# K with Q and V with U in one transformer block: four projections by seven block products each instead of eight

## The chip, the cores and the metric

The kernel runs on one core of a Trainium2 chip. The metric is the device time of one execution in microseconds (us), the median of several runs. Times in the trace are counted from the first instruction of one profiled execution. TensorE is written PE, its weight loads PEld, VectorE DVE, ScalarE ACT, GpSimd POOL and SyncE SP.

## What is computed

One layer of a hybrid block on 256 tokens of width 1024, all in fp32:

```
h    = rmsnorm(x)
proj = h @ w_in        # columns: q 512 | k 512 | v 512 | index q 256 | index k 64 | index weight 4 | u 512 | gates 2048
score[t, s] = sum over 4 index heads of relu(iq[t] . ik[s]) * iw[t]      # keys of the token's 64-chunk and before
the 64 highest scores choose the keys that token t may attend to
y_attn = attention(norm(q), norm(k), v) over the chosen keys, 8 heads of 64
y_pool = trailing means of u (windows 2, 4, 8, 16) minus u, times pool_w, bias, scale
x = x + (sig(gA) * (y_attn @ wA) + sig(gB) * (y_pool @ wB)) @ w_out
x = x + mixture of 32 experts, 4 per token (each 1024 -> 2048 -> 1024)
```

A token of the first 64 has exactly 64 admissible keys, so all of them are chosen, whatever its scores are.

## The kernel before, in words

**Stages.** The first 205 us hold the norms, the projections, the attention, the pooling and the router. From there a loop over the 32 experts reads 12 MB of weights for each, 400 MB in all, through a ring of ten slots of 2 MB in SBUF, and multiplies. The first of these loads is issued when the second half of the attention's product is made (`attn_ps`), the next when the gates' last product is made, and so on up to the output projection: the loads wait for slots which the first stage uses for its own weights and scratch.

**Order.** Nothing is scheduled by a program. Each engine has one hand-written list of instructions and runs it in order; semaphores (`s["..."]`) tie the lists together. An instruction that waits holds all that stand behind it on its engine.

**Loads.** SP issues, in this order, x, the index columns (two halves), then blocks of 2 MB: K, Q, V, U, four blocks of gates, the two branch matrices and w_out (`load_block`). There are six places for blocks; a block that takes the place of another waits until that one is used (`used`).

**Projections.** `index` (L1415, L1420) makes the index queries for all 256 tokens, transposed, and the index key with the index weights. `project` (L1442) makes K, Q and V: for each of two halves of the tokens eight matmuls of 128 tokens by 512 columns. U is made transposed (L1503), in 32 matmuls of 256 columns. A fp32 matmul shows as two records in the trace, a transpose as one.

**Seven products.** The gates and the two branches already use a scheme in which a product of 2 by 2 blocks takes seven block products instead of eight (`product`, L1531). For each piece four differences or sums of token blocks (`token_sums`, L1055 to L1058) and four differences of weight blocks (`weight_sum`, L1127) are made ahead; products 5, 6, 7 and 4 read them. The partial results 1, 6 and 5 are copied out of PSUM by ACT (`keep1`, `keep2`, `keep5`), and DVE adds them to the later ones (`gate_sum`, L1149). These finished corners are told by `c11_ok`, `c12_ok` and `c22_ok`. Product 4 starts only when `c22_ok` says that its PSUM bank has been read.

**Index scores.** DVE makes the scores of 128 tokens in one `tensor_scalar` (L1070) and three `scalar_tensor_tensor` (L1072) of two SBUF operands each, then eight rounds of `max` and `match_replace` (L1078, L1079), and this for both halves of the tokens; L1081 makes the mask. Before, this stands in DVE's list between the norm of K's heads and the norm of Q's heads (`norm_heads`, L1040 to L1044), while PE projects Q and V.

**Pooling.** POOL waits for U (`uT_sb`), scales it by the norm (L717) and makes the sums and differences of four windows (L724 to L731), 20 instructions. DVE's copy of the first attention result (`attn_out(0)`, L1137) waits for the end of that (`diff_ok`), because it writes where U stood. The corners of the gates stand behind it on DVE, and product 4 of the first gate piece waits for one of them.

Of the kernel before, what the change touches and what calls it, by code (L numbers as in the profile page):

```python
# [20 lines left out]
ALU = mybir.AluOpType  # L21
# [3 lines left out]
P = 128  # L25
BANK = 512
EPS = 1e-6
CHUNK = 64
# [12 lines left out]
def block_kernel(nc, x, attn_norm_g, w_in, q_norm_g, k_norm_g, pool_w, pool_b, pool_scale,  # L41
# [23 lines left out]
    assert T == 2 * P and D == 1024 and DA == BANK and HD == 64 and FE == D and E == 32  # L65
    assert P % CHUNK == 0 and 2 * CHUNK == P and TOPK == CHUNK
# [19 lines left out]
    with ExitStack() as ctx:  # L86
# [16 lines left out]
        kn = scratch(SUMS, 0, TT * DA).rearrange("p (a n) -> p a n", a=TT)  # L103
        qn = scratch(SUMS, 1024, TT * DA).rearrange("p (a n) -> p a n", a=TT)
        qT = scratch(SUMS, 2048, KA * T).rearrange("p (k t) -> p k t", k=KA)
        kT = scratch(SUMS, 3072, KA * T).rearrange("p (k t) -> p k t", k=KA)
# [8 lines left out]
        iwT = score[0:IH, 0:T]  # L115
        probs = [scratch(PROBS, H * KEY_AT[tt], H * KEYS[tt]).rearrange("p (h n) -> p h n", h=H) for tt in range(TT)]
        probsT_early, probsT_late = scratch(PROBS, H * KEYS_ALL, 2 * BANK), scratch(PROBS, 0, 2 * BANK)
# [4 lines left out]
        squares, diffT, pooledT, v = (work[:, 0], work[:, 1:3], work[:, 3:5], work[:, 5:7])  # L122
        diffT = diffT.rearrange("p a (b t) -> p (a b) t", b=2)
        pooledT = pooledT.rearrange("p a (b t) -> p (a b) t", b=2)
        uT = xn[:, 0, :].rearrange("p (g t) -> p g t", g=G)
        sumT = xn[:, 1, :].rearrange("p (g t) -> p g t", g=G)
# [10 lines left out]
        g2_rows = work[0:KD // W1_ROWS, 7, 0:W1_ROWS * P]  # L137
# [58 lines left out]
        def tail_in(e, c, i):  # L196
# [7 lines left out]
            idx_ps ik_sb iw_ps idx_sb iw_sb k_ps q_ps kq_sq kq_ss kq_rms kq_norm dots_ps relu_ok mask_ok v_ps v_sb kT_ps kT_sb qT_ps qT_sb logit_ps masked negmax prob_ok uT_ps uT_sb  # L204
            gate_sb prob_share probT_ps probT_sb attn_ps attnT_sb diff_ok
            token_sum weight_sum product_ps kept_sb
# [55 lines left out]
        def logit_ps(tt, h):  # L262


            if tt == 0:
                return bank[4 + h % 2][:, (h // 2) * P:(h // 2 + 1) * P]
            return bank[(2 if h % 2 == 0 else 0) + h // 4][:, (h // 2 % 2) * T:(h // 2 % 2 + 1) * T]
# [11 lines left out]

        def piece_weights(p):  # L280

            if p < 2:
                lo, hi = block_w(B_G0 + 2 * p, BANK), block_w(B_G0 + 2 * p + 1, BANK)
                return lo[:, 0:KD // 2, :], hi[:, 0:KD // 2, :], lo[:, KD // 2:KD, :], hi[:, KD // 2:KD, :]
            return quarters(block_w(B_WA + p - 2, D, KA), KA // 2, BANK)

        def piece_tokens(p):

            a11, a21, a12, a22 = quarters(hT if p < 2 else (attnT, pooledT)[p - 2], (KD if p < 2 else KA) // 2, P)
            return a11, a12, a21, a22  # L290

        def piece_sums(p):

            a, t = (hS, wide_t) if p < 2 else ((attnS, pooledS)[p - 2], branch_t[p - 2])
            return [a[:, i] for i in range(4)], t

        PIECE_BANKS = ((2, 3, 4), (5, 4, 3), (2, 6, 7), (5, 3, 4))
        PIECES = len(PIECE_BANKS)

        PRODUCTS = [(0, n) for n in (1, 5, 2, 6, 3, 7, 4)] + [(1, n) for n in (1, 5, 2, 6, 3, 7, 4)] + [  # L300
            (2, n) for n in (1, 5, 2, 6, 3, 7)] + [(3, 1), (2, 4)] + [(3, n) for n in (5, 2, 6, 3, 7, 4)]
        WEIGHT_SUMS = ((0, 1), (0, 2), (0, 3), (1, 1), (0, 4), (1, 2), (1, 3), (2, 1), (2, 2), (1, 4), (3, 1), (3, 2), (2, 3), (3, 3),
                       (2, 4), (3, 4))
# [5 lines left out]
        def weight_summed(p, i):  # L309
            return s["weight_sum"], WEIGHT_SUMS.index((p, i)) + 1  # L310

# [3 lines left out]
        def gate_cols(p, half):  # L315
            return slice(p * D + half * BANK, p * D + (half + 1) * BANK)
# [211 lines left out]
        def _(sp):  # L528
# [3 lines left out]
            def used(i):  # L532

                done, n = {B_IDX: (s["idx_ps"], 2), B_K: (s["k_ps"], TT), B_Q: (s["q_ps"], TT), B_V: (s["v_ps"], TT),
                           B_U: (s["uT_ps"], 2), B_G0: product_made(0, 4), B_G0 + 1: product_made(0, 4), B_G0 + 2: product_made(1, 4),
                           B_G0 + 3: product_made(1, 4), B_WA: product_made(2, 4), B_WP: product_made(3, 4),
                           B_WO: (s["out_ps"], TT + 1), B_WO + 1: (s["out_ps"], 2 * TT + 1)}[i]
                sp.wait_ge(done, n)
# [157 lines left out]
        def _(pool):  # L696
# [15 lines left out]

            pool.wait_ge(s["uT_sb"], 2)
            pool.wait_ge(s["inv_ok"], 1)
            pool.wait_ge(s["inv_row"], 1)
            for g in range(G):
                nc.gpsimd.tensor_tensor(uT[:, g, :], uT[:, g, :], inv_row, ALU.mult).then_inc(pool_step, 1)  # L717
                chain.n += 1
            pool.wait_ge(pool_step, chain.n)
# [16 lines left out]
        def _(act):  # L736
# [36 lines left out]
            nc.scalar.copy(iqT[:, :, :], bank[4][:, :].rearrange("p (b t) -> p b t", b=2)).then_inc(s["idx_sb"], 1)  # L773
            act.wait_ge(s["idx_ps"], 2)
            nc.scalar.copy(iwT, bank[5][ID:ID + IH, 0:T]).then_inc(s["idx_sb"], 1)
            act.wait_ge(s["iw_ps"], 1)
            act.wait_ge(s["x_inv"], 3 * TT)
            for tt in range(TT):
                nc.scalar.activation(iw[:, tt, :], bank[6][:, tt * IH:(tt + 1) * IH], ACT.Copy, scale=inv_iw(tt)).then_inc(s["iw_sb"], 1)
# [9 lines left out]

            for tt in range(TT):  # L790
                act.wait_ge(s["k_ps"], tt + 1)
                square_heads(tt, bank[tt][:, :], tt)

# [6 lines left out]
            for tt in range(TT):  # L800
                act.wait_ge(s["q_ps"], tt + 1)
                square_heads(TT + tt, bank[6 + tt][:, :], tt)
# [3 lines left out]
            for tt in range(TT):  # L806
                act.wait_ge(s["v_ps"], tt + 1)
                nc.scalar.activation(v[:, tt, :], bank[2 + tt][:, :], ACT.Copy, scale=inv_rms(tt)).then_inc(s["v_sb"], 1)
            for tt in range(TT):
                act.wait_ge(s["negmax"], tt + 1)  # L810
                for h in range(H):
                    nc.scalar.activation(prob(tt, h), prob(tt, h), ACT.Exp, bias=neg_max[:, tt, h:h + 1],
                                         accum_out=den[:, tt, h:h + 1]).then_inc(s["prob_ok"], 1)
            for b in range(2):
                act.wait_ge(s["uT_ps"], b + 1)
                nc.scalar.copy(uT[:, 2 * b:2 * b + 2, :], bank[6 + b][:, :].rearrange("p (g t) -> p g t", g=2)).then_inc(s["uT_sb"], 1)

            def keep1(p):
                act.wait_ge(*product_made(p, 1))
                if p:  # L820
                    act.wait_ge(s["c11_ok"], p)
                nc.scalar.copy(kept1, bank[PIECE_BANKS[p][0]][:, :]).then_inc(s["kept_sb"], 1)

            def keep2(p):
                act.wait_ge(*product_made(p, 6))
                if p:
                    act.wait_ge(s["c12_ok"], p)
                nc.scalar.copy(kept2, bank[PIECE_BANKS[p][0]][:, :]).then_inc(s["kept_sb"], 1)

            def keep5(p):  # L830
                act.wait_ge(*product_made(p, 5))
                if p:
                    act.wait_ge(s["c22_ok"], p)
# [1129 lines left out]
```

## Time and profile before

| | us |
|---|---|
| median of 3 runs | 1107.56 (1107.39 to 1108.15) |
| the profiled execution, its own time | 1106.32 |
| span of that execution in the trace | 1104.5 |
| PE busy | 1066.1 (97% of the span) |
| DVE busy | 251.9 (23%) |
| ACT busy | 171.0 (15%) |
| POOL busy | 23.8 (2%) |
| moved by DMA | 432.57 MB, 392 GB/s over the span |

The granted clock of PE is 1.000 over the span. The profiled execution is 1.24 us below the median of the runs.

### The profile page before, as it was taken

The page shows a single profiled execution, that of the slowest core. Times are in us where ns is not written, and L with a number is a line of the kernel's source. Part 1 is how long each engine was busy: PE and PEld are TensorE (multiplying, and loading weights), DVE is VectorE, ACT ScalarE, POOL GpSimd, SP SyncE. Part 2 cuts the span into 40 slices and gives each one's busy share as a digit, 9 for nine tenths or more (in the row PEclk, how much of TensorE's full clock was granted, in tenths as well). Part 3 has the DMA queues.
Part 4 walks back from the last instruction along what each step waited for, and adds up shares of the span by engine and source line. Part 5 has one row for each costly group of instructions (what it writes and reads, how often), then busy time and mean ns, then how long its engine had stood idle before and what let it go on. Part 6 is the DMA issues. An engine that isn't in the chain of part 4 may idle for free.

```text
span 1104.5 us, 11794 instructions
## 1 busy us (share of the span) xinstructions
PE 1066.1 (97%) x4914; PEld 418.9 (38%) x4914; DVE 251.9 (23%) x553; ACT 171.0 (15%) x378; POOL 23.8 (2%) x38
## 2 busy tenths in 40 slices
PE   9999999999999999999999989999899999999998
PEld 6474445533333333333333333333233333333332
DVE  3764451311112111111111111111111111111111
ACT  2143222111011111111111111111011111111112
POOL 0007000000000000000000000000000000000000
PEclk9999999999999999999999999999999999999999
DMA  9922678799999999999999999999999999999997
GB/s 339 375 84 76 229 304 343 306 426 427 426 411 421 436 430 433 422 437 432 431 432 429 435 428 436 428 436 427 434 431 431 432 433 432 430 433 433 426 428 286
DMA packets 34314, 432.57 MB, mean 392 GB/s; under 512 B 3548, under 2 KB 5104, under 8 KB 17648
## 3 DMA queue, kind: packets, MB, share of 16 engines
q1 hardware_dynamic: 32096, 430.73, 92.7%
q10 hardware_dynamic: 2192, 1.48, 0.5%
q8 instruction: 19, 0.31, 0.1%
q14 instruction: 7, 0.06, 0.0%
HBM read 431.15 MB, written 1.05 MB: 391 GB/s over the span
## 4 chain that ended last, share of the span: by engine, by line
PE 63%; DMA 33%; POOL 2%; DVE 1%; issue 0%; SPq 0%; POOLq 0%; ACT 0%; DVEq 0%
DMA ring<-in_expert_w_dram 33%; PE bank L455 24%; PE bank L484 14%; PE bank L1531 5%; PE bank L1442 4%; PE bank L493 4%; PE bank L418 3%; PE bank L1651 2%; PE bank L445 2%; PE bank L1503 1%; PE bank L432 1%; PE bank L467 1%; PE bank L1415 1%; PE bank L437 1%; DMA ring<-in_w_in_dram 1%
## 5 line engine op out<-in xcount | busy, mean ns | idle before, releaser
L455 PE MATMUL bank<-ring,work 128*64 128x512 f32 x2048 | 449.8, 594 | 16.5 <-DMA ring<-in_expert_w_dram 16.4
L455 PEld LDWEIGHTS bank<-ring,work 128*64 128x64 f32 x2048 | 142.9, 137 | 319.8 <-issue 287.1
L484 PE MATMUL bank<-ring,work 128*64 128x512 f32 x992 | 219.5, 593 | 12.3 <-DMA ring<-in_expert_w_dram 12.3
L484 PEld LDWEIGHTS bank<-ring,work 128*64 128x64 f32 x992 | 75.2, 137 | 152.2 <-issue 149.9
L1289 DVE TENSOR_SCALAR work<-bank 128x512 f32<-128x512 f32 x31 | 21.5, 692 | 458.3 <-PE bank L455 458.3
L924 ACT ACTIVATE work<-work 128x512 f32<-128x512 f32 x31 | 19.5, 630 | 481.0 <-DVE work L1289 481.0
L519 DVE TENSOR_TENSOR work<-bank,vecs 128x512 f32<-128x512 f32 x31 | 21.4, 691 | 213.5 <-PE bank L432 213.5
L493 PE MATMUL bank<-work,putT 64*128 64x512 f32 x248 | 61.9, 616 | 0.0
L418 PE MATMUL bank<-xs,pick 128*64 128x512 f32 x248 | 58.5, 592 | 0.0
L1531 PE MATMUL bank<-ring 128*128 128x512 f32 x112 | 49.5, 595 | 2.6 <-DVE ring L1149 2.6
L944 ACT COPY work<-bank 128x512 f32<-128x512 f32 x31 | 18.2, 587 | 205.8 <-PE bank L484 205.8
L1442 PE MATMUL bank<-ring 128*128 128x512 f32 x96 | 42.3, 595 | 0.0
L474 ACT COPY work<-bank 64x256 f32<-64x256 f32 (+1 forms) x112 | 40.2, 359 | 3.7 <-PE bank L467 2.6
L445 PE MATMUL bank<-b_rows,bias_pick 32*64 32x512 f32 x256 | 34.8, 613 | 0.0
L1531 PEld LDWEIGHTS bank<-ring 128*128 128x128 f32 x112 | 20.9, 190 | 26.7 <-issue 23.8
L418 PEld LDWEIGHTS bank<-xs,pick 128*64 128x64 f32 x248 | 17.7, 137 | 35.0 <-issue 35.0
L1127 DVE TENSOR_TENSOR ring<-ring 128x2048 f32<-128x2048 f32 (+1 forms) x16 | 28.5, 1781 | 10.1 <-PE bank L1531 8.7
L493 PEld LDWEIGHTS bank<-work,putT 64*128 64x128 f32 x248 | 21.3, 186 | 19.4 <-issue 15.8
L1651 PE MATMUL bank<-ring,xn 128*128 128x512 f32 (+1 forms) x80 | 28.6, 508 | 0.0
L510 DVE TENSOR_SCALAR put<-slot_id,place,weight 128x128 f32<-128x128 f32 x64 | 19.3, 344 | 37.6 <-PE bank L437 37.5
L1299 DVE TENSOR_TENSOR work<-work 128x512 f32<-128x512 f32 x26 | 27.4, 1053 | 0.9
L1442 PEld LDWEIGHTS bank<-ring 128*128 128x128 f32 x96 | 17.9, 190 | 21.0 <-issue 20.9
(239 smaller groups left out, 552.5 us busy)
## 6 DMA issues: line engine op xcount, KB each, us to landing
ring<-in_expert_w_dram SPq DMA_DIRECT2D x70, 4096.0 KB, 39.5
ring<-in_expert_w_dram SPq DMA_DIRECT2D x43, 2048.0 KB, 14.2
ring<-in_w_in_dram SPq DMA_DIRECT2D x8, 2048.0 KB, 20.9
ring<-in_expert_w_dram SPq DMA_DIRECT2D x13, 1024.0 KB, 10.3
ring<-in_w_out_dram SPq DMA_DIRECT2D x2, 2048.0 KB, 11.2
ring<-in_w_branch_attn_dram SPq DMA_DIRECT2D x1, 2048.0 KB, 7.9
ring<-in_w_branch_pool_dram SPq DMA_DIRECT2D x1, 2048.0 KB, 7.7
work<-in_expert_w_dram SPq DMA_DIRECT2D x2, 1024.0 KB, 13.0
```

What stands on the lines that cost most here:

```text
L418: mm = pe.matmul(ps_gather[SLOTS * half:SLOTS * (half + 1), :], pick[:, tt, :], xs[:, tt, half * BANK:(half + 1) * BANK], start=(tt == 0), ...
L445: mm = pe.matmul(dst, bias_pick[rows, :], b1_rows[rows, :], start=first, stop=not first, skip_group_check=True)
L455: mm = pe.matmul(dst, hTe[:, at:at + SLOTS], w[a][:, col:col + BANK], start=(k == 0 and not bias_first), stop=(k == KD - 1 and bias_first) ...
L474: last = nc.scalar.copy(dst[halves(h), :].rearrange("p (j i s) -> p i j s", i=2, s=SLOTS)[:, i, blocks, :], src[halves(i), :].rearrange("p ...
L484: mm = pe.matmul(ps[SLOTS * half:SLOTS * (half + 1), :], actT[:, at:at + SLOTS], w[a // 2][:, col:col + BANK], start=(k == 0), stop=(k == ...
L493: mm = pe.matmul(acc[2 * tt + half][:, :], at[rows, tt * P:(tt + 1) * P], src[rows, :], start=False, stop=True, skip_group_check=True)
L1127: nc.vector.tensor_tensor(out, x, y, ALU.subtract).then_inc(s["weight_sum"], 1)
L1289: nc.vector.tensor_scalar(gate_e, ps_gate[:, :], SWIGLU_LIMIT, None, ALU.min).then_inc(gate_ok, 1)
L1299: nc.vector.tensor_tensor(by_rows(act_e), lin, sig, ALU.mult).then_inc(glu_ok, 1)
L1442: mm = pe.matmul(dst, hT[:, k, tt * P:(tt + 1) * P], w[:, k, :], start=(k == 0), stop=(k == KD - 1))
L1531: mm = pe.matmul(ps, a[:, k, :], b[:, k, :], start=(start and k == 0), stop=(k == K - 1), skip_group_check=True)
L1651: mm = pe.matmul(ps, mergedT[:, k, tt * P:(tt + 1) * P], w[:, k, at:at + cols.stop - cols.start], start=(k == 0), stop=(k == KD - 1))
```

## The change

- K and Q become one piece of seven products (KQ), V and U another (VU). Both token halves and both matrices come out of one piece: K and V are the left columns, Q and U the right ones. The second half of the tokens of K, and of V, comes out of product 4.
- Of the eight weight differences, one (KQ, 1) is made by DVE; seven are made by POOL, each 128 x 2048 (`early_sum`). POOL waits for block V and U before (VU, 1), and for product 2 of VU before (VU, 4).
- The index queries are made for tokens 64 to 255 (192 columns); ACT fills the first 64 with a copy of others, since they don't matter.
- U is now made with tokens in partitions, scaled by the norm in DVE's sum, and transposed by PE (8 transposes). POOL's scaling of U goes.
- DVE's list: the token sums come ahead of the index key; then the difference (KQ, 1), the first corner of K and its norm, then the index scores and the choice of keys, then the other corners of KQ and their norms. Product 4 of KQ waits for `c22_ok`, the last of these corners.
- The logits of the attention are put between products of VU, and the first two weight differences of the gates ahead of DVE's copies of qT.
- `attn_out(0)` and its wait for `diff_ok` stand behind the three corners of the first gate piece.

On GpSimd, ahead of the pooling:

```diff
+            pool.wait_ge(*weight_summed(KQ, 1))
+            early_sum(KQ, 2)
+            early_sum(KQ, 3)
+            pool.wait_ge(*product_made(KQ, 2))
+            early_sum(KQ, 4)
+            pool.wait_ge(*block_landed(B_V))
+            pool.wait_ge(*block_landed(B_U))
+            pool.wait_ge(*product_made(KQ, 5))
+            early_sum(VU, 1)
+            pool.wait_ge(*product_made(KQ, 6))
+            early_sum(VU, 2)
+            early_sum(VU, 3)
+            pool.wait_ge(*product_made(VU, 2))
+            early_sum(VU, 4)
             pool.wait_ge(s["uT_sb"], 2)
             pool.wait_ge(s["inv_ok"], 1)
-            pool.wait_ge(s["inv_row"], 1)
-            for g in range(G):
-                nc.gpsimd.tensor_tensor(uT[:, g, :], uT[:, g, :], inv_row, ALU.mult).then_inc(pool_step, 1)
```

On VectorE:

```diff
+            dve.wait_ge(*block_landed(B_K))
+            dve.wait_ge(*block_landed(B_Q))
+            weight_sum(KQ, 1)
+            head_sum(kn[:, 0, :], 0, 0, s["c11_ok"])
+            norm_heads(0, kn[:, 0, :], kn[:, 0, :])
 
             dve.wait_ge(s["iw_sb"], TT)
...
                                     ALU.is_gt, ALU.mult).then_inc(s["mask_ok"], 1)
-            for tt in range(TT):
-                norm_heads(TT + tt, bank[6 + tt][:, :], qn[:, tt, :])
+            head_sum(qn[:, 0, :], 0, 1, s["c12_ok"])
+            head_sum(qn[:, 1, :], 1, 1, s["c22_ok"])
+            norm_heads(1, bank[0][:, :], kn[:, 1, :])
+            norm_heads(2, qn[:, 0, :], qn[:, 0, :])
+            norm_heads(3, qn[:, 1, :], qn[:, 1, :])
...
+            scaled_sum(v[:, 0, :], 0, 0, s["c11_ok"])
+            dve.wait_ge(*block_landed(B_G0))
+            dve.wait_ge(*block_landed(B_G0 + 1))
+            dve.wait_ge(*product_made(VU, 5))
+            dve.wait_ge(*weight_summed(VU, 2))
+            weight_sum(GA, 1)
+            dve.wait_ge(*product_made(VU, 6))
+            dve.wait_ge(*weight_summed(VU, 4))
+            weight_sum(GA, 2)
             for tt in range(TT):
                 dve.wait_ge(s["qT_ps"], tt + 1)
...
+            gate_sum(GA, 0, 1, s["c12_ok"])
+            weight_sum(GP, 3)
+            gate_sum(GA, 1, 1, s["c22_ok"])
             dve.wait_ge(s["diff_ok"], G)
             attn_out(0)
-            gate_sum(0, 0, 1, s["c12_ok"])
-            weight_sum(1, 3)
-            gate_sum(0, 1, 1, s["c22_ok"])
             attn_out(1)
```

On TensorE, whose new order for the two pieces this is (`transpose_kq` waits for all four norms):

```diff
             def product_4(p):
-                if p < 2:
+                if p < WA:
                     pe.wait_ge(s["c22_ok"], p + 1)
...
+            product_1(KQ)
...
+            product_2(KQ)
...
+            product_5(KQ)
+            product_6(KQ)
+            product_3(KQ)
+            product_7(KQ)
+            product_4(KQ)
+            product_1(VU)
+            product_2(VU)
+            product_5(VU)
+            product_6(VU)
...
+            pe.wait_ge(s["kq_norm"], 2 * TT)
+            for n in range(2 * TT):
+                transpose_kq(n)
+            product_3(VU)
...
+            attention_logits(0)
+            product_7(VU)
+            pe.wait_ge(s["c11_ok"], 2)
+            attention_logits(1)
+            product_4(VU)
...
+                    mm = pe.transpose(bank[4 + g // 2][:, at:at + P], u[:, tt, g * P:(g + 1) * P], ident[:, :])
...
+            product_1(GA)
```

The index scores' matmuls (`dots_ps`) stand between products 2 and 5 of KQ.

## Rows read from the trace of the kernel before

**Rows 1.** Windows: busy time of PE, PEld, DVE, ACT, POOL; clock; DMA share; GB/s

```profile
82.00:118.00 36.00, 33.43 (x137) 17.05 (x136) 12.21 (x9) 9.91 (x16) 21.34 (x24) 1.00 0.29 100
161.00:205.00 44.00, 43.82 (x206) 27.75 (x206) 13.86 (x42) 13.06 (x28) 0.00 (x0) 1.00 0.74 285
240.00:330.00 90.00, 90.00 (x431) 31.49 (x428) 13.55 (x30) 8.39 (x16) 0.00 (x0) 1.00 1.01 422
690.00:780.00 90.00, 85.43 (x410) 29.99 (x408) 14.39 (x30) 10.91 (x24) 0.00 (x0) 1.00 1.01 433
```

**Rows 2.** Timeline of PE: start, us, line, operation, count, idle before it

```profile
1.59 2.93 PE L1397 MATMUL bank<-ident 128*128 128x128 f32 x12 [1.59 <-POOL ident L699]
...
6.41 0.83 PE L1397 MATMUL bank<-ident 128*128 128x128 f32 x6
8.00 3.69 PE L1415 MATMUL bank<-ring 128*128 128x256 f32 x16 [0.76 <-DMA ring<-in_w_in_dram]
...
18.88 7.03 PE L1442 MATMUL bank<-ring 128*128 128x512 f32 x16
...
33.12 1.58 PE L1458 MATMUL bank<-ring 64*128 64x128 f32 x16
...
67.62 14.08 PE L1503 MATMUL bank<-ring 128*128 128x256 f32 x64
81.53 10.46 PE L1531 MATMUL bank<-ring 128*128 128x512 f32 x24
91.83 1.04 PE L1510 MATMUL bank<-ident,ring 128*128 128x128 f32 x8
...
108.71 7.13 PE L1531 MATMUL bank<-ring 128*128 128x512 f32 x16 [2.57 <-DVE ring L1149]
```

**Rows 3.** Issues of blocks Q and U on SP's queue, each with its time to landing

```profile
L560 SPq DMA_DIRECT2D ring<-in_w_in_dram x1: 3148/3148/3148, 3.3 to 3.3; - x1
...
DMA to landing us min/median/max: 20.1/20.1/20.1
...
L560 SPq DMA_DIRECT2D ring<-in_w_in_dram x1: 7122/7122/7122, 11.5 to 11.5; - x1
...
DMA to landing us min/median/max: 23.5/23.5/23.5
```

**Rows 4.** Timeline of DVE

```profile
28.39 0.69 DVE L1044 TENSOR_TENSOR ring<-bank,head_ss 128x512 f32<-128x512 f32 x1
...
35.75 0.28 DVE L1070 TENSOR_SCALAR ring<-ring,iw 128x128 f32<-128x128 f32 x1
...
53.42 0.68 DVE L1040 TENSOR_REDUCE head_ss<-work 128x8 f32<-128x512 f32 x1
...
76.87 2.29 DVE L1127 TENSOR_TENSOR ring<-ring 128x2048 f32<-128x2048 f32 x1
...
88.77 2.56 DVE L1127 TENSOR_TENSOR ring<-ring 128x2048 f32<-128x2048 f32 x1 [6.84 <-PE bank L1531]
92.10 0.69 DVE L1149 TENSOR_TENSOR ring<-bank,work 128x512 f32<-128x512 f32 x1 [0.78 <-PE bank L1531]
```

**Rows 5.** Timeline of POOL

```profile
82.40 2.78 POOL L717 TENSOR_TENSOR xn<-xn,put 128x256 f32<-128x256 f32 x4 [78.70 <-ACT xn L816]
...
85.39 1.89 POOL L726 TENSOR_TENSOR xn<-xn 128x1020 f32<-128x1020 f32 x1
...
88.46 0.73 POOL L731 TENSOR_TENSOR work<-work,xn 128x256 f32<-128x256 f32 x1
89.12 2.25 POOL L724 COPY work<-xn 128x6 f32<-128x6 f32 x1
91.34 1.45 POOL L726 TENSOR_TENSOR work<-xn 128x762 f32<-128x762 f32 x1
...
103.81 0.72 POOL L731 TENSOR_TENSOR work<-work,xn 128x256 f32<-128x256 f32 x1
```

**Rows 6.** Timeline of ACT

```profile
26.47 0.60 ACT L785 ACTIVATE work<-bank 128x512 f32<-128x512 f32 x1
```

More of the change, by code:

```diff
@@ L799, in _ @@
                     nc.scalar.activation(dst, src, ACT.Relu, scale=inv_dot(tt)).then_inc(s["relu_ok"], 1)
-            for tt in range(TT):
-                act.wait_ge(s["q_ps"], tt + 1)
-                square_heads(TT + tt, bank[6 + tt][:, :], tt)
+            keep5(KQ)
+            keep2(KQ)
+            act.wait_ge(*product_made(KQ, 4))
+            square_heads(1, bank[0][:, :], 1)
+            keep1(VU)
+            act.wait_ge(s["c12_ok"], 1)
+            square_heads(2, qn[:, 0, :], 0)
+            act.wait_ge(s["c22_ok"], 1)
+            square_heads(3, qn[:, 1, :], 1)
+            keep5(VU)
+            keep2(VU)
             for tt in range(TT):
@@ L805, in _, with exponentials @@
                 nc.scalar.copy(kT[:, :, tt * P:(tt + 1) * P], bank[tt][:, :].rearrange("p (k t) -> p k t", k=KA)).then_inc(s["kT_sb"], 1)
[L806 to L809, printed above, removed]
+            def exponentials(tt):
                 act.wait_ge(s["negmax"], tt + 1)
@@ L813, in _ @@
                                          accum_out=den[:, tt, h:h + 1]).then_inc(s["prob_ok"], 1)
+            exponentials(0)
+            act.wait_ge(*product_made(VU, 4))
+            nc.scalar.activation(v[:, 1, :], bank[2][:, :], ACT.Copy, scale=inv_rms(1)).then_inc(s["v_sb"], 1)
             for b in range(2):
                 act.wait_ge(s["uT_ps"], b + 1)
[L816 to L833, printed above, removed]
[L834 removed]
+                nc.scalar.copy(uT[:, 2 * b:2 * b + 2, :], bank[4 + b][:, :].rearrange("p (g t) -> p g t", g=2)).then_inc(s["uT_sb"], 1)
+            exponentials(1)
             def sigmoid(p, tt, half, ready, n):
@@ new lines, in product_6, with product_3, product_7, product_4 @@
+            def product_6(p):
+                pe.wait_ge(*kept(p, 1))
+                pe.wait_ge(*weight_summed(p, 2))
+                product(p, 6)
+            def product_3(p):
+                pe.wait_ge(*kept(p, 5))
+                product(p, 3)
+            def product_7(p):
+                pe.wait_ge(*kept(p, 6))
+                pe.wait_ge(*weight_summed(p, 3))
+                product(p, 7)
+            def product_4(p):
+                if p < WA:
+                    pe.wait_ge(s["c22_ok"], p + 1)
+                else:
+                    pe.wait_ge(s["c22_read"], p - GP)
+                pe.wait_ge(*weight_summed(p, 4))
+                product(p, 4)
@@ L1520, in attend @@
                 mm.then_inc(s["attn_ps"], 1)
-            def product(p, n):
-                x, y, w = (bank[b][:, :] for b in PIECE_BANKS[p])
-                (a11, a12, a21, a22), (b11, b12, b21, b22) = piece_tokens(p), piece_weights(p)
-                (s1, s2, s3, s4), (t1, t2) = piece_sums(p)
-                a, b, ps, start = {1: (a11, b11, x, True), 5: (s1, t1, y, True), 2: (a12, b21, w, True), 6: (s2, t2, x, False),
-                                   3: (s4, b22, y, False), 7: (s3, b12, x, False), 4: (a22, b21, x, False)}[n]
-                K = a.shape[1]
-                for k in range(K):
-                    mm = pe.matmul(ps, a[:, k, :], b[:, k, :], start=(start and k == 0), stop=(k == K - 1), skip_group_check=True)
-                mm.then_inc(s["product_ps"], 1)
```

497 lines of the change are left out of this document (258 added, 239 removed).

## The prediction

> **What bounds the kernel now.** I read the windows first. From 240 us on the DMA engines are full (share 1.01 and 422 GB/s, later 433), and at 690 us PE already has gaps in 90 us, so the expert loop ends when its weights have landed [rows 1]. Between 161 and 205 us the DMA share is only 0.74: there the loads wait for slots that PE frees, and PE has no gaps [rows 1]. So what the first stage gains or loses on PE moves the start of the full stream, and the end, by the same amount. Then the timeline of PE: it runs without a gap from the first projection at 18.88 us up to one stall of 2.57 us before 108.71 [rows 2]. That first stage is to be added up. The critical resources are PE and, as it turns out, whatever stands in front of a semaphore in DVE's list.
>
> **What PE saves.** Eight matmuls of 128 x 512 (16 records) of K take 18.88 to 25.75 us, 6.87 [rows 2]; K, Q and V are six such groups, and U takes 13.9 (the 14.08 of its row less the tail that the next row overlaps) [rows 2]: 55.5 us. A block product of four matmuls is half of such a group, 3.43 (three in a row: 10.46) [rows 2]; fourteen make 48.0. That is 7.5 less. The index queries are 16 matmuls of 256 columns, 32 records; 16 records take 3.5 [rows 2], so all 7.0, and a quarter fewer columns save 1.7. Eight transposes for u cost 0.9 (the 1.04 of eight less the tail) [rows 2]. Together **-8.3**.
>
> **The copy moved later.** The 2.57 us stall waited for a corner sum that stood behind `diff_ok` on DVE. Now the corner goes first. `diff_ok` itself comes about 20 us after U is in place (POOL from 85.2 to 104.5) [rows 5], with the first gate piece, about 28 us, as cover, and who reads the attention result waits another 20. So **-2.6**, and nothing later. Were that cover gone, it would cost the 2.6 again.
>
> **The new wait: product 4 of KQ.** It needs `c22_ok`, and DVE gives that only behind the whole choice of keys. PE's side: the index ends at 17.2 (18.88 less 1.7), then products 1 and 2, the small transposes, 1.5 of dots [rows 2], and products 5, 6, 3, 7: 17.2 + 6 x 3.43 + 0.2 + 1.5 = 39.5, with 0.35 of small waits **39.8**. DVE's side: block Q is issued at 3.3 and lands 20.1 later [rows 3], 23.4. The difference (KQ, 1) takes 2.29 [rows 4], the corner of K 0.69, a head norm 2.6 (from the square at 26.47 to the end of the product with the inverse at 29.08) [rows 4, 6]: 29.0. The choice of keys takes 35.75 to 53.42 us, 17.7 [rows 4]; then two corners of 0.66: **48.0**. Even with DVE undisturbed PE stands 8.2 us, where the choice of keys was covered by Q and V before.
>
> **And DVE is disturbed.** POOL makes its differences in just that stretch. What both engines do when they meet shows twice in one place: DVE's difference of 88.77 takes 2.56 instead of 2.29, which is as if it began 0.15 before POOL's instruction of 88.46 ends; and POOL's next one, a copy of six elements, takes 2.25 and ends with DVE's [rows 4, 5]. Each keeps the other out for its whole length. DVE's corner at 92.10, with one operand in PSUM, takes its usual 0.69 beside a running POOL instruction [rows 4, 5]. In the choice of keys L1070 and L1072 have their tensors in SBUF, and the three L1072 of a half have two each; so has now the last step of K's norm, since K no longer lies in PSUM.
> The Trainium skill, SBUF — State Buffer, section "Who interferes with whom", says so as a rule: a VectorE instruction with two SBUF inputs, or a single-input one in its two-port mode, and a GpSimd instruction that reads SBUF shut each other out for the full instruction. The trace agrees for `tensor_tensor`; for `scalar_tensor_tensor` no row shows it.
> How long is a POOL difference of 2048 elements? 1020 took 1.89 and 762 took 1.45, so 1.67 ns an element more, and 2048 makes **3.6** [rows 5]. Ends: 2.3, as fast as DVE does it [rows 4], and 5.6 as eight pieces of 0.70 (2.78 for four of 256) [rows 5]. I take 3.6, by the nearest row.
> POOL begins at 25.8, after DVE's difference. Its instructions end at about 29.4, 33.5, 37.6, then (VU, 1), whose block U landed at 35.0 (11.5 + 23.5) [rows 3], at 41.5, then 45.3 and 49.1; the seventh waits for a product of VU. DVE meets them so: the norm's last step waits 0.9, the scaling of the first half 3.45, then, as a POOL instruction gets in between each one or two of DVE's, a sum 3.45 and another 3.45; eight rounds of `max` run free beside POOL; the second half waits once, 1.3. That is 12.5 us, and `c22_ok` comes at 60.6. **PE stands 20.8 us**, plus 0.35 before.
>
> **Behind it.** PE's logits wait for qT. DVE has, from the vector transposes on, 0.65 + 0.66 + two differences of 2.24 + two copies of 0.7, 7.2 us, against 5.2 on PE (four groups of transposes, product 3): **+2.1**. The transposes wait for the four norms, but under products 1, 2, 5 and 6 of VU (13.7 us) they fit. SP's loads of the later gate blocks now wait for product 4 of KQ, and land some 10 us behind it, 30 us ahead of their use. ACT's exponentials of the second half fall beside the first gate piece, 13 us before their readers; nothing. Later DVE work only keeps its order.
>
> **The clock.** In the trace PE's idle products ran at 0.24 us each at the start (12 in 2.93), later six in 0.83 [rows 2]: coming from rest cost about 1.5 us. After 2.57 us of rest nothing was lost (the next 16 records took the usual 7.13) [rows 2]. After 8 or 20 us I expect the low level. Ends: 0, or 3.4 if all of product 4 runs at half speed. I take **+1.5**.
> The Trainium skill, TensorE: Matmul & The Clock Gate, Part 1, calls rest the throttled default and says activity lifts it; by it the 1.5 belongs in the sum, without it the sum is 1.5 lower.
>
> **Sum.** -8.3 - 2.6 + 20.8 + 0.35 + 2.1 + 1.5 = **+13.9 us**. On the profiled execution's 1106.3 that is 1120.2; the median lies 1.24 above it, so 1121.5. A measurement of this kernel can tell about 0.2%, 2.2 us.
>
> **Rivals.**
> *A, the engines don't shut each other out here* (L1072 and L1070 run beside POOL). Place: the wait for `c22_ok`; price then 8.2 instead of 20.8: the sum is +1.3 with the clock's 1.5, -0.2 without, 1107.4 to 1108.9. Not slower by what can be told. It decides if DVE loses less than about 3 us to POOL. For it: no row has the two together. Against: the two places where they met [rows 4, 5]. Chance 0.19, 0.16 of it within 0.2% and 0.03 above.
> *B, as A, and Q lands early.* A block takes 5.8 us in the queue (Q lands at 23.4, U, two blocks on, at 35.0) [rows 3]; if Q came half a block earlier, at 20.6, the stall would shrink by as much, and without a clock fall the sum is -3.0, 1104.6. It needs Q before 21.4. Against: the loads ahead and the queue don't change, and the trace says 23.4. Chance 0.09.
> *C, POOL's differences are longer.* Each further 0.9 us on one lengthens the stall by about 5.4. At 5.6 the stall is near 33 and the time 1133. Chance 0.14.
> The Trainium skill, GPSIMD Engine Reference, section 3, gives 4497 ns for this shape (fp32 `tensor_tensor`, 2048 elements). By it the estimate would be about 1127 instead of 1121.5.
>
> **How the numbers follow.** The forecast's own case has 0.58, spread from 1113 (2.3 us a difference, or only one half of the scores blocked, no clock loss) to 1127. With C it makes 0.72, all slower; with A's 0.03, 0.75. Same 0.16, faster 0.09. The range from 1107.5 to 1129 leaves out B, the lower edge of A and the long end of C.
>
> **What would show it.** Right: a PE gap of 15 to 27 us before product 4 of KQ, released by DVE's corner sum; L1070 and L1072 durations of up to 3.5 us instead of 0.3 to 0.5, or gaps before them, each ending with a POOL row; POOL rows of about 3.6 us; the gap of 2.57 us gone; the expert loop unchanged, only shifted. Wrong: L1072 at 0.35 and 0.49 beside POOL, a gap of 8 us (A), Q landed early (B), or a change in the DMA-bound stretch of a size other than the shift of PE at its start, which would make the first paragraph wrong.

## The result and the profile after

| | us |
|---|---|
| before, median of 4 runs | 1107.47 (1106.97 to 1108.15) |
| after, median of 4 runs | 1129.42 (1129.03 to 1130.69) |
| ratio | 1.0202, 95% interval 1.0187 to 1.0217 |
| the profiled execution of after, its own time and span | 1129.03, 1127.2 |

The change costs 22.0 us. The direction was forecast, the size was not: 1121.5 stood there, with a range up to 1129.0. The busy line of the page of the profile has PE at 1066.3 us, as before (1066.1), so the time that was added is rest. Windows of after (columns as in [rows 1]):

```profile
40.00:72.00 32.00, 6.20 (x12) 2.56 (x11) 24.91 (x59) 0.46 (x1) 13.06 (x3) 0.63 0.13 47
...
60.00:66.00 6.00, 0.00 (x0) 0.00 (x0) 5.65 (x18) 0.00 (x0) 0.00 (x0) 0.50 0.00 0
66.00:72.00 6.00, 5.58 (x10) 2.56 (x11) 0.37 (x1) 0.46 (x1) 0.00 (x0) 0.73 0.00 0
...
240.00:330.00 90.00, 89.92 (x438) 31.77 (x436) 17.87 (x39) 10.82 (x20) 0.00 (x0) 1.00 1.01 428
```

The expert loop is as it was [rows 1]; the loss is in the first row, where PE works 6 us of 32. PE's timeline of after, beside [rows 2]:

```profile
4.64 3.49 PE L1480 MATMUL bank<-ident,xs 128*128 128x128 f32 x16
...
17.74 3.60 PE L1520 MATMUL bank<-ring 128*128 128x512 f32 x8
...
26.62 14.00 PE L1520 MATMUL bank<-ring 128*128 128x512 f32 x32
66.42 18.82 PE L1520 MATMUL bank<-ring 128*128 128x512 f32 x40 [25.80 <-DVE xn L1127]
...
93.17 2.08 PE L1633 MATMUL bank<-ring 64*128 64x128 f32 x16 [2.21 <-DVE ring L1181]
95.18 4.37 PE L1520 MATMUL bank<-ring 128*128 128x512 f32 x8
99.47 2.00 PE L1633 MATMUL bank<-ring 64*128 64x256 f32 x16
...
105.97 10.54 PE L1520 MATMUL bank<-ring 128*128 128x512 f32 x24
...
130.64 7.13 PE L1520 MATMUL bank<-ring 128*128 128x512 f32 x16
```

The first gate piece starts at 105.97 instead of 81.53: +24.4. Its two rests are 28.0 us together, of which the products saved take a part back. The 2.57 us rest inside the gate piece is gone (130.64 has none), so from there on the shift is 21.9. What holds up the corner sum that ends the 25.80 us is seen when POOL's and DVE's timelines of after are laid side by side (POOL first):

```profile
25.31 14.09 POOL L729 TENSOR_TENSOR ring<-ring 128x2048 f32<-128x2048 f32 x3 [21.63 <-DVE ring L1115]
39.58 13.71 POOL L729 TENSOR_TENSOR ring<-ring 128x2048 f32<-128x2048 f32 x3 [0.17 <-POOL ring L729]
78.46 4.51 POOL L729 TENSOR_TENSOR ring<-ring 128x2048 f32<-128x2048 f32 x1 [25.17 <-PE bank L1520]
```

```profile
22.94 2.29 DVE L1115 TENSOR_TENSOR ring<-ring 128x2048 f32<-128x2048 f32 x1 [4.06 <-DMA ring<-in_w_in_dram]
...
27.97 2.42 DVE L1102 TENSOR_TENSOR xn<-xn,head_ss 128x512 f32<-128x512 f32 x1
30.31 4.53 DVE L1144 TENSOR_SCALAR ring<-ring,iw 128x128 f32<-128x128 f32 x1
34.87 13.98 DVE L1146 SCALAR_TENSOR_TENSOR ring<-ring,iw 128x128 f32<-128x128 f32 x3
49.07 0.30 DVE L1152 MAX8 top<-ring 128x8 f32<-128x128 f32 x1
...
55.20 1.52 DVE L1146 SCALAR_TENSOR_TENSOR ring<-ring,iw 128x256 f32<-128x256 f32 x3
...
79.40 4.12 DVE L1102 TENSOR_TENSOR xn<-xn,head_ss 128x512 f32<-128x512 f32 x1
```

Six POOL differences run back to back from 25.31 to 53.29, one every 4.66 us (4.5 of them its own). The norm's last step (0.69 alone), the scaling (0.28 alone, [rows 4]) and the three sums (0.37 each alone) each end within 0.6 us of the end of one of them: 1.7 + 4.3 + 12.9 = 18.9 us lost in five instructions. `max` runs beside the sixth at its usual 0.3, and the second half's sums find POOL idle. The seventh difference, at 78.46, holds the last norm (4.12 instead of 0.69), where nobody waits: the transposes that need it start at 85.56.

### The profile page after: what moved, and what is told of

It is laid out like the page before. It is cut to its first block, busy times and chain, and to the rows that moved or that the text cites. A ratio compares the mean times of both kernels' runs of the same rounds, so it can differ in the third digit from the quotient of the medians.

```text
span 1127.2 us, 11758 instructions
## 1 busy us (share of the span) xinstructions
PE 1066.3 (95%) x4874; PEld 413.0 (37%) x4874; DVE 282.3 (25%) x560; ACT 174.0 (15%) x384; POOL 58.1 (5%) x41
## 4 chain that ended last, share of the span: by engine, by line
PE 60%; DMA 34%; DVE 4%; issue 1%; SPq 0%; ACT 0%; DVEq 0%
DMA ring<-in_expert_w_dram 32%; PE bank L466 23%; PE bank L495 13%; PE bank L1520 9%; PE bank L504 3%; PE bank L429 3%; PE bank L1733 2%; PE bank L456 2%; DMA ring<-in_w_in_dram 2%; DVE ring L1146 1%; PE bank L443 1%; PE bank L478 1%; DVE ring L1153 1%; PE bank L448 1%; DVE ring L1115 1%
## 5 line engine op out<-in xcount | busy, mean ns | idle before, releaser
L1520 PE MATMUL bank<-ring 128*128 128x512 f32 x224 | 101.4, 606 | 25.8 <-DVE xn L1127 25.8
L1520 PEld LDWEIGHTS bank<-ring 128*128 128x128 f32 x224 | 42.5, 194 | 76.5 <-issue 49.4
L729 POOL TENSOR_TENSOR ring<-ring 128x2048 f32<-128x2048 f32 x7 | 31.9, 4552 | 47.4 <-PE bank L1520 25.2
L1115 DVE TENSOR_TENSOR ring<-ring 128x2048 f32<-128x2048 f32 (+1 forms) x17 | 31.4, 1844 | 7.1 <-DMA ring<-in_w_in_dram 4.1
L1366 DVE SCALAR_TENSOR_TENSOR work<-work 128x512 f32<-128x512 f32 x31 | 21.4, 692 | 1.5
## 6 DMA issues: line engine op xcount, KB each, us to landing
ring<-in_w_in_dram SPq DMA_DIRECT2D x8, 2048.0 KB, 20.8
work<-in_expert_w_dram SPq DMA_DIRECT2D x2, 1024.0 KB, 12.9
```

The source lines that it names most:

```text
L729: nc.gpsimd.tensor_tensor(out, x, y, ALU.subtract).then_inc(s["early_sum"], 1)
L1115: nc.vector.tensor_tensor(out, x, y, ALU.subtract).then_inc(s["weight_sum"], 1)
L1520: mm = pe.matmul(ps, a[:, k, :], b[:, k, :], start=(start and k == 0), stop=(k == K - 1), skip_group_check=True)
```

## The experiments

Eleven kernels, each run beside the kernel before. The first five edit the changed kernel.

**GpSimd writes, but reads nothing.** The values of q, k, v and u are therefore not those of the change.

```diff
-                nc.gpsimd.tensor_tensor(out, x, y, ALU.subtract).then_inc(s["early_sum"], 1)
+                nc.gpsimd.memset(out, 0.0).then_inc(s["early_sum"], 1)
```

> The seven weight differences on GpSimd are replaced by instructions of the same size that only write zeros, so that they read nothing (the values of q, k, v and u are wrong by that). Theory: VectorE and GpSimd shut each other out while both read SBUF; then L1144 takes 0.3 and each of the three L1146 of the first half 0.35 again instead of 4.5 and 4.7, the choice of keys takes 17.7 us instead of 34.8, the stall before product 4 of KQ is 8 to 9 us instead of 25.8, and the time is 1129.4 less 17 = about 1112. Rival 1, any GpSimd instruction blocks, whether it reads or writes: the DVE rows stay as long as the write instruction is, some 2 us each, and the time is near 1120. Rival 2, the DVE rows are long for another reason than GpSimd (the loads that land meanwhile): nothing changes, 1129.

Measured: 1112.42 us, ratio 1.0043 (1.0026 to 1.0060). POOL's, DVE's and PE's timelines of this kernel:

```profile
26.39 5.59 POOL L729 MEMSET ring<- 128x2048 f32 x3 [22.70 <-DVE ring L1115]
```

```profile
29.53 0.61 DVE L1144 TENSOR_SCALAR ring<-ring,iw 128x128 f32<-128x128 f32 x1
30.17 1.13 DVE L1146 SCALAR_TENSOR_TENSOR ring<-ring,iw 128x128 f32<-128x128 f32 x3
```

```profile
48.90 19.36 PE L1520 MATMUL bank<-ring 128*128 128x512 f32 x40 [8.51 <-DVE xn L1127]
```

17.0 of the 22 us go with POOL's reads. The three sums stand beside the third memset and take 1.13 us, as without POOL. The largest part of what is left comes from the order of the work: a rest of 8.51 us, which the prediction had priced at 8.2. Behind it the rest of 2.2 us ahead of the logits and slower products stay.

**The two corners between the halves of the choice.**

```diff
+                if tt == 0:
+                    head_sum(qn[:, 0, :], 0, 1, s["c12_ok"])
+                    head_sum(qn[:, 1, :], 1, 1, s["c22_ok"])
...
-            head_sum(qn[:, 0, :], 0, 1, s["c12_ok"])
-            head_sum(qn[:, 1, :], 1, 1, s["c22_ok"])
```

> Only VectorE's order is changed: the two corner sums of KQ that product 4 waits for stand between the two halves of the choice of keys. Theory (the stall is the length of what stands before the second corner in DVE's list, GpSimd's part included): the corner comes about 10.3 us earlier, since the second half of the choice takes 54.8 to 65.1, the stall goes from 25.8 to about 15.5, and the time to 1119. The three norms then run under products 1, 2, 5 and 6 of VU as before or make a small stall. Rival (the second half only moves and comes due before the transposes): the gain is taken back at the wait for the four norms, and the time stays near 1129.

Measured: 1120.32 us, ratio 1.0112 (1.0096 to 1.0129). The rest is 15.64 us instead of 25.80. So 10 us of it is the second half of the choice, which the corners need not wait for.

**GpSimd's three later differences held back until the mask is made.**

```diff
             pool.wait_ge(*product_made(KQ, 5))
+            pool.wait_ge(s["mask_ok"], 1)
             early_sum(VU, 1)
```

> GpSimd waits for the mask before its first difference for VU; the three for KQ stay where they are. Theory (each GpSimd difference that is ready during the first sums costs DVE one whole length, 4.5 to 4.7 us): two of the four long DVE rows become short, the corner comes about 9.3 us earlier, the stall is near 16.5, the time near 1120, or up to 3 us more if the norms of Q now meet the later differences. Rival (what counts is not how often they meet, but that GpSimd runs at all, for instance a slow-down by its memory traffic): the DVE rows shorten all alike, and the gain is in proportion to the overlap, 3 to 5 us.

Measured: 1121.52 us, ratio 1.0124 (1.0107 to 1.0141). DVE's timeline:

```profile
31.24 4.53 DVE L1145 TENSOR_SCALAR ring<-ring,iw 128x128 f32<-128x128 f32 x1
35.80 5.47 DVE L1147 SCALAR_TENSOR_TENSOR ring<-ring,iw 128x128 f32<-128x128 f32 x3
```

With three differences pending there are three meetings: the norm, the scaling and one sum. The other two sums have 0.4 us each, and the rest shrinks to 17.39. This shows the count: one DVE instruction held for each difference that is pending. The differences that were moved meet two norms of Q instead (1.64 and 3.72 us), under PE's products.

**Idle products in the two rests.** PE gets 110 idle products before product 4 and 8 before the first logits; nothing else is changed.

```diff
+            pe.wait_ge(s["c11_ok"], 1)
+            idle_product(110)
             product_4(KQ)
...
+            pe.wait_ge(s["vec_ok"], 4)
+            idle_product(8)
```

> 110 products of no use are put on TensorE before product 4 of KQ (about 24 us at 0.217 each, inside the 25.8 us stall) and 8 before the first logits. Theory: after both stalls the clock had fallen; 1.6 us were lost in the five products behind the first, 2.0 in the logits and the product behind the second; with TensorE kept busy these rows come back to 17.2 and 0.93 + 3.5, and the time is about 3.5 us lower, 1126. Rival: the long rows behind the stalls have another cause (operands, queue), nothing changes in them, 1129.4.

Measured: 1126.17 us, ratio 1.0172 (1.0155 to 1.0189): 3.3 us less, of which the rows give 3.0 to the clock (granted 1.00 in this profile from 60 to 72 and from 88 to 100 us). PE's timeline:

```profile
66.34 17.43 PE L1520 MATMUL bank<-ring 128*128 128x512 f32 x40 [1.38 <-DVE xn L1127]
...
91.71 1.16 PE L1637 MATMUL bank<-ring 64*128 64x128 f32 x16 [0.43 <-DVE ring L1181]
92.80 3.70 PE L1520 MATMUL bank<-ring 128*128 128x512 f32 x8
96.43 2.00 PE L1637 MATMUL bank<-ring 64*128 64x256 f32 x16
```

These are the durations at the full clock. Against them after loses 1.4 us in the five products (18.82), and 1.6 from the first logits to the second: 99.47 - 93.17 = 6.30, here 96.43 - 91.71 = 4.72.

**The gate's two differences behind the mask of the logits.**

```diff
-            weight_sum(GA, 1)
...
-            weight_sum(GA, 2)
...
             mask_logits(0)
+            weight_sum(GA, 1)
             scaled_sum(u[:, 1, :], 1, 1, s["c22_ok"])
             mask_logits(1)
+            weight_sum(GA, 2)
```

> The changed kernel, with VectorE's two gate weight sums of the first group put behind the two mask operations of the logits, so that the logits of the first tokens no longer wait for them. My theory: the idle time of 2.21 us ahead of the first logits' products is from VectorE's queue, and the 2.0 us that TensorE loses just behind it (2.08 and 4.37 us where 0.93 and 3.60 are usual) are the clock's answer to it; both go, so 1129.4 - 2.2 - 2.0 = about 1125.2 us, with 0.9 us for the first 16 logits products. First rival: the clock falls anyway there, from the long stall before it: 1127.2. Second rival: the gate's products wait for their late sums, and nothing is gained: 1129.

Measured: 1126.14 us, ratio 1.0169 (1.0153 to 1.0184). PE's timeline:

```profile
66.55 19.90 PE L1520 MATMUL bank<-ring 128*128 128x512 f32 x40 [25.91 <-DVE xn L1127]
...
92.10 1.16 PE L1633 MATMUL bank<-ring 64*128 64x128 f32 x16
93.19 3.70 PE L1520 MATMUL bank<-ring 128*128 128x512 f32 x8
```

The rest ahead of the logits and the slow products behind it are gone. It is 0.9 short of the forecast: in this profile the five products behind the long rest took 19.90 us, 1.1 more than in after, though the list up to there is the same.

**The later copy alone, then with the queries for 192 tokens, in the kernel before.**

```diff
-            dve.wait_ge(s["diff_ok"], G)
-            attn_out(0)
             gate_sum(0, 0, 1, s["c12_ok"])
             weight_sum(1, 3)
             gate_sum(0, 1, 1, s["c22_ok"])
+            dve.wait_ge(s["diff_ok"], G)
+            attn_out(0)
```

> The kernel before with one part of the change alone: the copy of the first difference's product, and the tick that lets it be read, moved behind the four corner sums. My theory: the stall that the kernel before had ahead of the logits (2.57 us) goes and nothing takes its place, so 1107.6 - 2.6 = about 1105.0 us. Rival: the corner sums or the copy are needed a step later and the stall only moves: 1107.6 within 0.5.

> The kernel before with the later copy and the index queries for 192 tokens, so two of the small parts of the change without the seven products of K, Q, V and U. My theory: 1105.0 for the copy, less 1.7 us for the shorter index projection, = about 1103.3 us. Rival: TensorE's shorter start is given back where it waits for the weight sums of K: 1105.0.

Measured: 1104.94 us, ratio 0.9974 (0.9965 to 0.9983), and 1102.86 us, ratio 0.9958 (0.9944 to 0.9972). These two small parts of the change are worth 2.9 us, and 2.1 us more. (The stall that goes stood in the gate piece, not ahead of the logits as the first expectation says.) PE's timeline of the second has no rest from its first projection to the first gate piece, and gives the prices of the old K, Q, V and U:

```profile
17.57 7.03 PE L1444 MATMUL bank<-ring 128*128 128x512 f32 x16
...
80.23 10.46 PE L1533 MATMUL bank<-ring 128*128 128x512 f32 x24
```

**GpSimd kept apart from VectorE's two-operand work.** Of the eight differences VectorE now makes three, all of K with Q, and GpSimd five. The rest of the change is kept, in this order:

```diff
-            pool.wait_ge(*weight_summed(KQ, 1))
-            early_sum(KQ, 2)
-            early_sum(KQ, 3)
+            pool.wait_ge(*weight_summed(KQ, 3))
             pool.wait_ge(*product_made(KQ, 2))
             early_sum(KQ, 4)
...
             early_sum(VU, 2)
+            pool.wait_ge(s["kq_norm"], 2 * TT)
             early_sum(VU, 3)
...
             head_sum(kn[:, 0, :], 0, 0, s["c11_ok"])
+            weight_sum(KQ, 2)
             norm_heads(0, kn[:, 0, :], kn[:, 0, :])
...
+            weight_sum(KQ, 3)
...
+            choose_keys(0, 5)
             head_sum(qn[:, 0, :], 0, 1, s["c12_ok"])
             head_sum(qn[:, 1, :], 1, 1, s["c22_ok"])
+            choose_keys(0, TOPK // 8 - 5)
+            choose_keys(1, TOPK // 8)
```

The scores of both halves are made ahead of `weight_sum(KQ, 3)`, ACT's `keep1(VU)` comes ahead of a square, and the gate's differences stand behind the masks.

> The changed kernel with its differences dealt so that GpSimd's never stand beside what VectorE hurries for: VectorE makes the first three of K with Q, the scores of both halves of the index are made ahead, GpSimd starts its one of K with Q only after VectorE's last weight sum there and its three of V with U only after the norms of K and Q, two corner sums are put between the rounds of the choice, and the gate's sums stand later as in the run of that name. My theory (the loss is GpSimd's and VectorE's turns on the same memory, not the seven products themselves): no stall of TensorE over 2 us ahead of the logits, the first gate product starts about 5 us earlier than the 81.5 us of the kernel before, and with the later copy 1107.6 - 5.5 - 2.6 = 1099.5, say 1098 to 1102 us. Rival: VectorE, which has more to do now, is the bound by itself; TensorE waits some 5 to 8 us for the norms or for the weight sums, and the time is 1105 to 1108.

Measured: 1099.34 us, ratio 0.9925 (0.9912 to 0.9939), the fastest of all. PE's, POOL's and DVE's timelines:

```profile
41.40 17.43 PE L1530 MATMUL bank<-ring 128*128 128x512 f32 x40 [0.85 <-DVE xn L1126]
...
75.70 10.54 PE L1530 MATMUL bank<-ring 128*128 128x512 f32 x24
```

```profile
36.08 4.52 POOL L729 TENSOR_TENSOR ring<-ring 128x2048 f32<-128x2048 f32 x1 [32.39 <-DVE ring L1114]
40.76 9.18 POOL L729 TENSOR_TENSOR ring<-ring 128x2048 f32<-128x2048 f32 x2 [0.17 <-POOL ring L729]
57.38 9.19 POOL L729 TENSOR_TENSOR ring<-ring 128x2048 f32<-128x2048 f32 x2 [7.44 <-DVE xn L1101]
```

```profile
30.22 1.12 DVE L1150 SCALAR_TENSOR_TENSOR ring<-ring,iw 128x128 f32<-128x128 f32 x3
...
59.54 2.38 DVE L1178 TENSOR_TENSOR qk_gain<-vecs 128x1 f32<-128x1 f32 x1
```

A POOL difference takes 4.5 us with nobody in its way, and the three sums are back at 1.12. One small product of 128 x 1 still meets POOL and is held 2.2 us (0.16 alone), beside PE's product 3.

**The gate's differences put back, in this arrangement.**

```diff
             scaled_sum(v[:, 0, :], 0, 0, s["c11_ok"])
+            weight_sum(GA, 1)
+            weight_sum(GA, 2)
...
             mask_logits(0)
-            weight_sum(GA, 1)
             scaled_sum(u[:, 1, :], 1, 1, s["c22_ok"])
             mask_logits(1)
-            weight_sum(GA, 2)
```

> The arrangement with GpSimd kept apart (1099.3 us), with the two gate weight sums put back ahead of the copies of qT, where the changed kernel has them. The question is what a short rest of TensorE costs when no long one stands before it. In the changed kernel the 2.2 us ahead of the logits were followed by 1.6 us of slower products, 38 us behind the rest of 25.8 us began to end; in the kernel before 2.57 us were followed by nothing. Theory one: the short rest alone costs only itself, 2.2 us, so about 1101.5 us, with 1.16 and 3.70 us for the 16 logits products and the product behind them. Theory two: such a rest in front of the logits costs another 1.6 us whatever stood before: about 1103.1 us, with the logits products at up to 2.1 us and the product behind them at 4.4 to 5.4.

Measured: 1109.08 us, ratio 1.0012 (1.0002 to 1.0021). Both theories missed, and the question on the clock was not answered, since the rest was 8 us and not 2.2. DVE's and PE's timelines:

```profile
60.09 2.39 DVE L1178 TENSOR_TENSOR qk_gain<-vecs 128x1 f32<-128x1 f32 x1
...
63.36 8.32 DVE L1114 TENSOR_TENSOR ring<-ring 128x2048 f32<-128x2048 f32 x2
```

```profile
73.15 2.08 PE L1643 MATMUL bank<-ring 64*128 64x128 f32 x16 [8.05 <-DVE ring L1191]
...
79.86 2.00 PE L1643 MATMUL bank<-ring 64*128 64x256 f32 x16
```

I had moved POOL's last two differences behind the norms and overlooked that the gate's differences would meet them there: two of DVE's took 8.32 us instead of 4.6, the small product 2.2 more, and with the 2.2 us that the changed kernel had there that is the 8.05. Another 2.0 us went to the clock (79.86 - 73.15 = 6.71 to the second logits, 4.72 usual). In this arrangement the place of two differences decides over 9.7 us.

**Three of the differences of K with Q on VectorE, and nothing else.** An edit of the changed kernel:

```diff
-            pool.wait_ge(*weight_summed(KQ, 1))
-            early_sum(KQ, 2)
-            early_sum(KQ, 3)
+            pool.wait_ge(*weight_summed(KQ, 3))
...
             head_sum(kn[:, 0, :], 0, 0, s["c11_ok"])
+            weight_sum(KQ, 2)
+            weight_sum(KQ, 3)
             norm_heads(0, kn[:, 0, :], kn[:, 0, :])
```

> The changed kernel with one part of that arrangement alone: VectorE makes the differences 1, 2 and 3 of K with Q one behind the other ahead of the norm, and GpSimd starts with the fourth; the index scores stay where they are. My theory (what counts is whether a GpSimd difference is pending when VectorE reaches its two-operand instructions, not how many there are): GpSimd's differences start at about 30.5 us, the norm's last step ends at about 35.7 instead of 30.3, the first scores are held by the two that follow until about 50.3, and are done at about 51.5 instead of 49.1. The wait ahead of product 4 is about 28 us, and the time 1129.4 + 2.4 = about 1132 us. Rival: with two differences of 4.6 us fewer on GpSimd the shutting out shrinks by as much, less what VectorE does itself: 1122 to 1125 us.

Measured: 1131.26 us, ratio 1.0209 (1.0194 to 1.0224). POOL's and DVE's timelines:

```profile
30.51 4.51 POOL L729 TENSOR_TENSOR ring<-ring 128x2048 f32<-128x2048 f32 x1 [26.82 <-DVE ring L1113]
35.23 13.91 POOL L729 TENSOR_TENSOR ring<-ring 128x2048 f32<-128x2048 f32 x3 [0.21 <-DMA ring<-in_w_in_dram]
```

```profile
31.63 3.94 DVE L1100 TENSOR_TENSOR xn<-xn,head_ss 128x512 f32<-128x512 f32 x1
35.49 4.53 DVE L1144 TENSOR_SCALAR ring<-ring,iw 128x128 f32<-128x128 f32 x1
40.05 9.63 DVE L1146 SCALAR_TENSOR_TENSOR ring<-ring,iw 128x128 f32<-128x128 f32 x3
```

Two differences fewer on POOL bring nothing. DVE reaches the norm's last step and its scores just as POOL begins its four, and four instructions are held. So the gain of the arrangement above isn't the dealing alone. There the scores were made before POOL had anything pending (30.22 against 36.08 us); that this is what it needs fits both kernels, but the scores made ahead alone were not run.

**A short rest alone.** In the arrangement with GpSimd kept apart:

```diff
+            pe.wait_ge(*weight_summed(VU, 4))
             attention_logits(0)
```

> The arrangement with GpSimd kept apart (1099.3 us), in which TensorE now waits ahead of the first logits for GpSimd's last difference, which ended at 66.6 us where the logits began at 64.5: a rest of some 2.1 us there with nothing else changed, and with no long rest before it. Theory one: it costs only itself, about 1101.4 us, the logits' first products at 1.16 us and the product behind them at 3.70. Theory two: a rest at this place costs another 1.6 to 2.0 us by the clock, as in the changed kernel: 1103.0 to 1103.4 us, with up to 2.1 and 4.4 to 5.4 us there.

Measured: 1101.92 us, ratio 0.9947 (0.9934 to 0.9961). PE's timeline:

```profile
66.80 1.16 PE L1643 MATMUL bank<-ring 64*128 64x128 f32 x16 [2.16 <-POOL ring L729]
67.89 5.40 PE L1530 MATMUL bank<-ring 128*128 128x512 f32 x8
73.22 2.00 PE L1643 MATMUL bank<-ring 64*128 64x256 f32 x16
```

By the trace theory two: 6.42 us to the second logits where 4.72 is usual, so 1.7 lost on top of 2.16, with no long rest before. The first gate product starts 4.0 us later (79.72 against 75.70). The time has only 2.6 of them, and lies nearer to theory one's 1101.4. From a group of transposes ahead of the expert loop (158.88 and 154.86 us) to the last products (1093.27 and 1091.04) the two profiled executions took 934.4 and 936.2 us, and the kernel before 934.9: a scatter of that stretch which I did not trace further. The granted clock in windows of this kernel:

```profile
66.80:68.00 1.20, 1.20 (x17) 1.08 (x17) 0.00 (x0) 0.00 (x0) 0.00 (x0) 1.00 0.00 0
69.00:71.00 2.00, 2.00 (x3) 0.73 (x3) 1.93 (x12) 0.86 (x5) 0.00 (x0) 0.50 0.00 0
```

It was still 1.00 in the rest and over the first logits, and 0.50 only behind them, in the middle of the next product.

## Why the direction was right and the size wrong

**What PE saves**, -8.3 forecast: near. With no disturbance it is seen in the arrangement with GpSimd kept apart, against the kernel with the copy and the queries alone. A block product took 3.51 us, not 3.43 (fourteen from start to start: 49.2 us). The 6.87 us of the group that I halved is no row: [rows 2] has 7.03 from its start to its end, and in the trace the next product starts 6.96 after it. The sum had a slip too: six times 6.87 and 13.9 are 55.1, not 55.5. Measured, the old projections are 55.7. So 6.5 and not 7.5. The index gave 1.7 as forecast, the transposes of u cost 1.0. Together -7.2.

**The copy**, -2.6: right, 2.9 by itself, and nothing came later.

**The wait for `c22_ok`**, +20.8: 25.8, the step that failed; of the 8.1 us between the forecast +13.9 and the result, 5.0 lie here. The cause held, and so did its first layer, 8.2 us (8.5 once POOL reads nothing). What was mis-sized is the time for which DVE is held: 12.5 forecast, 18.9 measured. Five meetings were forecast and five came, but
- each was sized by a difference of 3.6 us, where they take 4.5 by themselves and 4.66 in a row. I drew a line through 762 and 1020 elements [rows 5] and read it at 2048. Over the norm, the scaling and two sums that is 3.3 us;
- I let POOL in between "each one or two" of DVE's instructions and gave the last meeting to the second half, for 1.3 us. POOL got in before every one of the first half, and the fifth meeting held the third sum for a whole difference: 3.0 us more.

The rest grew by 5.0 and not by these 6.3, since DVE began 0.5 us earlier than forecast (22.94) and PE came to the wait 0.8 later (40.6 us).

The Trainium skill, GPSIMD Engine Reference, section 3, gives 4497 ns for this shape. The trace agrees, with 4.51 and 4.52 us; the estimate from it was about 1127 where mine was 1121.5. It would still have missed the fifth meeting. I had taken the extrapolation as the nearest row, though it went to twice the longest shape seen.

**The 0.35 of small waits** did not come here (26.62 follows with no idle time); in the profiles of the first three experiments it was 0.5, 1.7 and 1.4 us. **The wait before the logits**, +2.1: right, 2.2.

**The clock**, +1.5: 3.0. The long rest cost 1.4, as forecast, but with luck: behind the same rest the fifth experiment's kernel lost 2.5. The short one cost 1.6 more. I had read from the 2.57 us rest of [rows 2] that such a one is free.

**The start**, no term of mine: PE's first projection came 0.6 later than the shorter index explains, for 16 transposes took 3.49 us instead of 1.96. It is no part of the change: the same transposes took 2.83 and 2.51 us in the profiles of the kernels with the later copy, and what sets it was not tried. The granted clock reads 1.00 there, and also over the twelve idle products from which I had worked out the 1.5, so that column does not bear out my reading of them as the clock. The 0.6 probably cost nothing: it lies ahead of the long rest, and DVE's list up to the corner began with the landing of Q, so without it the rest would have been as much longer.

By the measured terms: -7.2 - 2.6 + 25.8 + 2.2 + 1.4 + 1.6 + 0.6 = +21.8, against 22.0.

**The rivals.** *A* (no shutting out) fell with the first experiment. Its wait of 8.2 us was right (8.51), its time was not: 1108.9 at most, where the kernel without the shutting out took 1112.42, for the clock and the smaller saving. *B* fell with the landing of Q: DVE's difference starts at 22.94, 0.5 earlier than forecast, not 2. *C* (longer POOL differences) was the nearest to what happened: 1.06 us more on each makes by its rule 6.4, and 5.0 came in the rest. That these are near is in part luck: the length made 3.3 and the count 3.0, which *C* did not have. The range stopped at 1129.0, because I put the long end of C outside it.

**Shown and open.** Shown: the shutting out (POOL's reads taken away), its count per pending difference, the place of the corners, the clock's share, the two small gains, and that seven products pay when POOL is kept apart: 1099.34 against 1102.86 for the small parts alone. Open: which parts of that arrangement are needed, the scores made ahead among them, and why the kernel before lost nothing after its 2.57 us. One difference stands in the rows and was not tried: there full products follow the rest, and at the other place the small products of the logits do.

## What to carry to other kernels

Before work is dealt to GpSimd, list what VectorE has to do beside it with two operands in SBUF, or in a `tensor_scalar`. Each such instruction, however small, may be held for one whole GpSimd instruction, so large GpSimd instructions belong beside `max`, `match_replace` or operations that read PSUM. A product saved pays only if what it newly waits for was already early: here a corner stood behind a choice of keys that had been covered until then. Price a shape by a row of that shape; a line drawn to twice the longest one seen needs both its ends in the range.

## What the runs showed of the hardware

- POOL and DVE took turns instruction by instruction. With n differences pending, n instructions of DVE were held, each until a difference ended (3 in the third experiment, 4 with three sums on VectorE, and 5 beside the changed kernel's 6, the sixth finding DVE at `max`). A product of 128 x 1 was held 2.2 us, a `tensor_scalar` of 128 x 128 4.3 us.
- A GpSimd memset of the same tiles (1.8 us each) held no two-operand instruction (three sums in 1.13 us), and a `tensor_scalar` once, for 0.3 us (0.61 instead of 0.28). The Trainium skill, SBUF — State Buffer, section "Who interferes with whom", says that a VectorE instruction with two SBUF inputs contends with a GpSimd instruction that reads SBUF, "not with one that only writes it". The trace agrees.
- What PE lost behind a rest had little to do with its length. Five products of 17.43 us took 19.36 after 8.5 us of rest, 20.00 after 15.6, 19.41 after 17.4 and 18.82, 19.90 and 20.03 after 25.8, 25.9 and 26.3, each in one profile. After 2.2 us of rest before the logits 1.6 to 1.7 us were lost, after 8.05 us 2.0, and after the 2.57 us of [rows 2] nothing. The granted clock stood at 0.50, the 1.2 GHz level, from 60 to 66 us in after, where PE rested, and at 0.73 over the 6 us behind (the windows above). In the last experiment it fell to 0.50 only behind the logits that followed the rest of 2.16 us.
